# Mixture-of-experts encoder layer, one core: the item loops end one item earlier, and the last item's rows and both partial sums are added by TensorE

## The chip, the core and the metric

The kernel runs on one core of a Trainium2 chip. The metric is the device time of one execution in microseconds, lower is better. TensorE (PE) multiplies matrices into PSUM, VectorE (DVE), ScalarE (ACT) and GpSimd (POOL) do the elementwise work, and SyncE (SP) issues most of the DMAs.

## The reference

One post-norm layer over 1024 tokens of width 1024. A mixing part (pooling, convolution and memory attention) gives `x`, and then:

```python
scores = sigmoid(xt @ w_router)
_, idx = top_k(scores + router_bias, 8)          # 64 experts
gates = sel / sum(sel) * 2.5
for each block of 128 token rows of one expert e:
    h = silu(xb @ w_gate[e]) * (xb @ w_up[e])    # 1024 -> 256
    y = (h @ w_down[e]) * g
    acc = acc.at[tok].add(y)
out = layer_norm(alpha * x + acc + shared_expert(x)) # g2, b2
```

The number of blocks depends on the data. All values are float32.

## The kernel before

The mixing part and the router run first. The expert part is a list of items, each of 128 token rows times one expert. Items 0 to 7 are the shared expert's tiles, whose results go to DRAM with plain DMAs. Items from 8 (`NT`) on are routed ones, and `n_items`, read from the router's table, is their end. In the profiled execution it is 103: 1236 down matmuls at 12 an item, and 2304 gate/up matmuls at 24 for each of the steps 8 to 103.

Each engine has its own loop over the items, two to an iteration (`step_pe`, `step_act`, `step_v`), ordered by semaphores. Step `i` on TensorE transposes the gathered rows of item `i+1` (`rows_transposed`), transposes the hidden tile of item `i-1`, does `gate_up(i)` (24 matmuls), and `down(i-1)` (12 matmuls). `step_act(i)` writes the output of item `i-2` from PSUM to `ysb`, slot `i` modulo 2 (line 917), and `step_v` forms the low halves of the split operands. The loops run while `n_items` is at least `i`, so the last step has `i = n_items`: its `gate_up` is of an item that does not exist, and its `down` is of the last real one. After the loop, ScalarE (line 985) and VectorE (line 1470) write one half each of the last item's `ysb`.

GpSimd runs `fetch`: it gathers rows (`xg`, line 647), loads an item's list of tokens and gates into `idx` (line 640), and adds an item's `ysb` to DRAM by an indirect DMA with addition (line 657). There are two partial sums in DRAM, `sum_d[0]` and `sum_d[1]`: items of even number add to one and odd items to the other. There are 95 such scatters.

The closing part: SyncE waits (line 495) until all scatters but the last have landed and loads the half that the last item does not touch into `early`, in two DMAs of 2 MB (line 502). It then waits until the last scatter has landed and all engines are done (line 504), and loads the other half, tile by tile, into `late_` (line 506, eight DMAs of 512 KB). TensorE adds both into PSUM with the identity as stationary operand, in plain float32 (`add_part`, line 1860), for six of the eight tiles of 128 tokens. Tiles 4 and 6 (`ADDED`) are added by VectorE (line 1509). The LayerNorm of each tile: for tiles 0 and 7 VectorE takes the moments (`moments`, line 1498); for tiles 1 to 6 ScalarE does, in two passes (lines 1002 to 1012). GpSimd forms the power -1/2 (line 696), and VectorE normalises in two passes (`normalise`, lines 1486, 1490 and 1493). SyncE stores the tile (line 509). PSUM has four pairs of banks for the tiles; tile `t` of 4 and later waits for the first pass of tile `t-4`.

Of the kernel before, what the change touches and what calls it, by code (L numbers as in the profile page):

```python
# [14 lines left out]
F = mybir.dt.float32  # L15
# [4 lines left out]
ALU = mybir.AluOpType  # L20
# [29 lines left out]
ADDED = (4, 6)  # L50
# [6 lines left out]
def build(nc, a, out):  # L57
# [9 lines left out]
    with ctx:  # L67
# [79 lines left out]
        early = at("early", 96, [128, NT, D])  # L147
        late_ = at("late_", 0, [128, NT, D])
# [138 lines left out]
        s_endR = sem("s_endR")  # L287

        s_early = [sem(f"s_early{n}") for n in range(2)]
        s_late = [sem(f"s_late{t}") for t in range(NT)]  # L290
# [3 lines left out]
        s_added = sem("s_added")  # L294
# [67 lines left out]
        def _(sp):  # L362
# [138 lines left out]
            for n in range(2):  # L501
                sp.dma_start(early[:, 4 * n:4 * n + 4], rows_of(past % 2, 4 * n, 4)).then_inc(s_early[n], 16)
            sp.wait_ge(s_endC, 3)
            sp.wait_ge(s_endR, 1)
            for t in range(NT):
                sp.dma_start(late_[:, t:t + 1], rows_of((past + 1) % 2, t, 1)).then_inc(s_late[t], 16)
# [7 lines left out]
        def _(g):  # L514
# [174 lines left out]
            past = g.value_load(nit[0:1, 1:2], min_val=E, max_val=MAX_ITEMS - NT)  # L689
            for s in range(2):  # L690
                g.wait_ge(s_xg[s], 16 * ((past + 5 - s) // 2))
                g.wait_ge(s_yd[s], 16 * ((past + 1 - s) // 2))
            g.sem_inc(s_endR, 1)
# [6 lines left out]
        def _(act):  # L700
# [268 lines left out]
            with act.Fori(0, GROUPS) as group:  # L969
                with act.If(n_items > 2 * GROUP * group + NT + 3):  # L970
                    with act.Fori(0, GROUP) as pair:
                        jj = GROUP * group + pair
                        with act.If(n_items > 2 * jj + NT + 3):
                            step_act(2 * jj + NT + 4, 0, jj + 1)
                            with act.If(n_items > 2 * jj + NT + 4):
                                step_act(2 * jj + NT + 5, 1, jj + 1)


            late = act.value_load(nit[0:1, 2:3], min_val=E - 2, max_val=MAX_ITEMS - NT - 2)
            act.wait_ge(s_yd[0], 16 * ((late + 1) // 2))  # L980
            act.wait_ge(s_yd[1], 16 * (late // 2))
            slot = (n_items + 1) % 2
            act.wait_ge(s_dn, n_items)
            gate = idx[:, bass.ds((n_items + RING - 1) % RING, 1), 2:3].bitcast(F).rearrange("p a n -> p (a n)")
            nc.scalar.activation(ysb[:, bass.ds(slot, 1), 0:512].rearrange("p a n -> p (a n)"), ps[:, 5, :], ACT.Copy,
                                 scale=gate).then_inc(s_y, 1)
# [5 lines left out]
            for n, t in enumerate(range(1, NT - 1)):  # L992
                s = t % 2
                if t in ADDED:
                    act.wait_ge(s_added, ADDED.index(t) + 1)
                    y = acc[:, t]
                else:
                    act.wait_ge(s_pc, t + 1 - len([u for u in ADDED if u < t]))
                    y = ps[:, 2 * (t % 4):2 * (t % 4) + 2, :].rearrange("p a n -> p (a n)")
# [17 lines left out]
        def _(v):  # L1017
# [371 lines left out]
            def item_tables_out():  # L1389
                v.wait_ge(s_tabp, 1)  # L1390
                step(V.tensor_copy(tab[:].rearrange("p a b -> p (a b)"),
                                   ps[0:1, 7, 0:3 * TAB]))
                step(V.tensor_copy(nit[0:1, 0:1], endE[0:1, NE - 1:NE]))
                step(V.tensor_scalar(nit[0:1, 1:2], endE[0:1, NE - 1:NE], float(NT), None, ALU.subtract))
                step(V.tensor_scalar(nit[0:1, 2:3], endE[0:1, NE - 1:NE], float(NT + 2), None, ALU.subtract))
                settle()
                v.sem_inc(s_tabs, 1)
# [58 lines left out]
            with v.Fori(0, GROUPS) as group:  # L1456
                with v.If(n_items > 2 * GROUP * group + NT - 1):
                    with v.Fori(0, GROUP) as pair:
                        jj = GROUP * group + pair
                        with v.If(n_items > 2 * jj + NT - 1):  # L1460
                            step_v(2 * jj + NT, 0)
                            with v.If(n_items > 2 * jj + NT):
                                step_v(2 * jj + NT + 1, 1)
            settle()
            v.wait_ge(s_h, n_items + 1)
# [3 lines left out]
            gate = idx[:, bass.ds((n_items + RING - 1) % RING, 1), 2:3].bitcast(F).rearrange("p a n -> p (a n)")  # L1469
            V.tensor_scalar(ysb[:, bass.ds((n_items + 1) % 2, 1), 512:D].rearrange("p a n -> p (a n)"), ps[:, 6, :],  # L1470
                            gate, None, ALU.mult).then_inc(s_y, 1)
# [4 lines left out]
            def summed(t):  # L1476
                if t in ADDED:
                    return acc[:, t]
                return ps[:, 2 * (t % 4):2 * (t % 4) + 2, :].rearrange("p a n -> p (a n)")
# [26 lines left out]
            def add(t):  # L1506
                v.wait_ge(s_early[t // 4], 16)
                v.wait_ge(s_late[t], 16)
                step(V.tensor_tensor(acc[:, t], early[:, t], late_[:, t], ALU.add))
                settle()  # L1510
                v.sem_inc(s_added, 1)

            for t in range(NT):
                if t + 2 in ADDED:
                    add(t + 2)
# [5 lines left out]
            v.wait_ge(s_pc, NT - len(ADDED))  # L1521
# [5 lines left out]
        def _(pe):  # L1527
# [318 lines left out]
            with pe.Fori(0, GROUPS) as group:  # L1846
                with pe.If(n_items > 2 * GROUP * group + NT - 1):
                    with pe.Fori(0, GROUP) as pair:
                        jj = GROUP * group + pair
                        with pe.If(n_items > 2 * jj + NT - 1):  # L1850
                            step_pe(2 * jj + NT, 0, jj + 1)
                            with pe.If(n_items > 2 * jj + NT):
                                step_pe(2 * jj + NT + 1, 1, jj + 2)
            pe.wait_ge(s_dn, n_items)
# [3 lines left out]
            def add_part(t, rows):  # L1858
                for h in range(2):
                    last = mm(ps[:, 2 * (t % 4) + h, :], ident[:], rows[:, t, h * 512:(h + 1) * 512],  # L1860
                              start=(rows is early), stop=(rows is late_))
                return last

            summed = [t for t in range(NT) if t not in ADDED]
            for t in summed[:4]:
                pe.wait_ge(s_early[t // 4], 16)
                add_part(t, early)
            for n, t in enumerate(summed):
                if n >= 4:
                    pe.wait_ge(s_acc, t - 3)  # L1870
                    pe.wait_ge(s_early[t // 4], 16)
                    add_part(t, early)
                pe.wait_ge(s_late[t], 16)
                add_part(t, late_).then_inc(s_pc, 1)
# [52 lines left out]
```

## Time and profile before

| | us |
|---|---|
| median of 3 runs | 1392.77 |
| lowest, highest | 1388.06, 1400.06 |
| profiled execution, its time | 1394.81 |
| profiled execution, its span | 1393.2 |
| PE busy | 1316.1 (94%) |
| DVE busy | 956.1 (69%) |
| ACT busy | 795.5 (57%) |
| POOL busy | 498.6 (36%) |

The span runs from the first to the last instruction of the profiled execution, and its time is 1.61 us more. A row of a timeline gives where an instruction, or several of one kind, began, and for how long they ran. What stands in brackets is the idle time of that engine ahead of them and what ended it. A float32 matmul leaves more than one record in the trace, so counts of records and of calls in the code are told apart below. The mean granted clock of TensorE over the span is 0.972 of full speed.

### The profile page before, as it was taken

The page shows a single profiled execution, that of the slowest core. Times are in us where ns is not written, and L with a number is a line of the kernel's source. Part 1 is how long each engine was busy: PE and PEld are TensorE (multiplying, and loading weights), DVE is VectorE, ACT ScalarE, POOL GpSimd, SP SyncE. Part 2 cuts the span into 40 slices and gives each one's busy share as a digit, 9 for nine tenths or more (in the row PEclk, how much of TensorE's full clock was granted, in tenths as well). Part 3 has the DMA queues.
Part 4 walks back from the last instruction along what each step waited for, and adds up shares of the span by engine and source line. Part 5 has one row for each costly group of instructions (what it writes and reads, how often), then busy time and mean ns, then how long its engine had stood idle before and what let it go on. Part 6 is the DMA issues. An engine that isn't in the chain of part 4 may idle for free.

```text
span 1393.2 us, 25748 instructions
## 1 busy us (share of the span) xinstructions
PE 1316.1 (94%) x6395; PEld 1088.1 (78%) x6396; DVE 956.1 (69%) x1109; ACT 795.5 (57%) x1055; POOL 498.6 (36%) x444
## 2 busy tenths in 40 slices
PE   8989877999988999999999999999999999999974
PEld 6877765788876888888888888888888888888851
DVE  5798884767663777775777556647669579777727
ACT  4122274232235777766777556647678578777724
POOL 0000164265572333433343334333433343343322
PEclk9999988899998999999999999999999999999988
DMA  6121203232358899988999789778889899999665
GB/s 245 34 88 61 112 40 120 85 92 62 107 168 303 314 330 299 334 297 246 307 338 350 240 238 320 233 225 277 298 275 357 257 337 334 332 330 319 185 190 228
DMA packets 77970, 324.13 MB, mean 233 GB/s; under 512 B 22560, under 2 KB 24768, under 8 KB 52720
## 3 DMA queue, kind: packets, MB, share of 16 engines
q1 hardware_dynamic: 43056, 251.05, 48.5%
q0 software_dynamic: 33728, 68.47, 21.0%
q10 hardware_dynamic: 1152, 4.19, 0.7%
q8 instruction: 17, 0.28, 0.1%
q14 instruction: 17, 0.14, 0.0%
HBM read 290.51 MB, written 67.72 MB: 257 GB/s over the span
## 4 chain that ended last, share of the span: by engine, by line
PE 81%; DMA 5%; DVE 5%; issue 2%; ACT 2%; POOL 2%; another core or an unknown queue 1%; ACTq 0%; SPq 0%; POOLq 0%; DVEq 0%
PE ps L1788 35%; PE ps L1806 18%; PE ps L1654 7%; PE ps L1533 6%; PE ps L1558 5%; PE ps L1734 3%; DMA raw<-in_w_up 3%; DVE cv L1118 2%; PE ps L1723 2%; PE ps L1819 1%; DMA xg<-x_d,idx 1%; PE ps L1570 1%; DMA sum_d<-ysb,idx 1%; DMA xin<-in_x 1%
## 5 line engine op out<-in xcount | busy, mean ns | idle before, releaser
L1788 PE MATMUL ps<-wgu,xTe 128*128 x2304 | 549.9, 394 | 1.9 <-ACT wgu L843 0.8
L1788 PEld LDWEIGHTS ps<-wgu,xTe 128*128 128x128 f32 x2304 | 426.3, 188 | 90.2 <-issue 5.0
L657 POOL DMA_INDIRECT sum_d<-ysb,idx x95 | 176.4, 1857 | 510.5 <-ACT ysb L917 439.0
L1806 PE MATMUL ps<-wdn,hT 128*128 (+1 forms) x1236 | 302.0, 394 | 0.1
L1401 DVE TENSOR_TENSOR wgu<-raw,wgu (+1 forms) x128 | 287.7, 2289 | 8.2 <-issue 3.4
L1806 PEld LDWEIGHTS ps<-wdn,hT 128*128 128x128 f32 x1236 | 234.3, 190 | 49.2 <-issue 0.6
L843 ACT CAST wgu<-raw (+1 forms) x128 | 247.0, 1930 | 2.4 <-SPq L445 2.3
L1406 DVE TENSOR_TENSOR xTe<-ps,xTe 128x512 fp32r<-128x512 f32 x194 | 124.6, 684 | 131.0 <-ACT xTe L912 131.0
L917 ACT ACTIVATE ysb<-ps,idx 128x512 f32<-128x512 f32 x188 | 119.3, 686 | 122.5 <-PE ps L1806 122.5
L1401 DVE TENSOR_TENSOR wdn<-raw,wdn x64 | 146.7, 2293 | 59.6 <-ACT wdn L905 59.6
L647 POOL DMA_INDIRECT xg<-x_d,idx x99 | 110.4, 1115 | 50.0 <-issue 35.0
L905 ACT CAST wdn<-raw x64 | 125.0, 1953 | 0.0
L963 ACT ACTIVATE hs<-ps 128x256 f32<-128x256 f32 x96 | 36.9, 384 | 145.0 <-PE ps L1788 145.0
L1558 PE MATMUL ps<-xT,whl 128*128 128x512 f32 x480 | 110.1, 390 | 0.0
L912 ACT CAST xTe<-ps 128x512 fp32r<-128x512 f32 x194 | 104.4, 598 | 4.3 <-PE ps L1533 3.9
L1558 PEld LDWEIGHTS ps<-xT,whl 128*128 128x128 f32 x480 | 89.9, 188 | 19.2 <-issue 0.4
L1654 PE MATMUL ps<-wo,mst 128*128 128x512 f32 x384 | 97.6, 415 | 7.0 <-POOL mst L551 4.3
L1533 PE MATMUL ps<-ident,xg 128*128 128x128 f32 x776 | 100.9, 273 | 2.2 <-issue 2.0
L1533 PEld LDWEIGHTS ps<-ident,xg 128*128 128x128 f32 x776 | 90.5, 140 | 15.3 <-issue 2.9
L1435 DVE TENSOR_TENSOR hx<-hs,ps 128x256 f32<-128x256 f32 x96 | 40.1, 418 | 89.7 <-ACT hs L963 89.7
L600 POOL DMA_INDIRECT list_d<-tg,addr x64 | 74.0, 1157 | 60.9 <-DVEq L1253 44.2
L1654 PEld LDWEIGHTS ps<-wo,mst 128*128 128x128 f32 x384 | 76.0, 201 | 23.8 <-issue 7.6
(230 smaller groups left out, 1162.9 us busy)
## 6 DMA issues: line engine op xcount, KB each, us to landing
raw<-in_w_gate SPq DMA_DIRECT2D x64, 1024.0 KB
raw<-in_w_up SPq DMA_DIRECT2D x64, 1024.0 KB
raw<-in_w_down SPq DMA_DIRECT2D x64, 1024.0 KB
wraw<-in_w_in SPq DMA_DIRECT2D x10, 512.0 KB, 3.3
xin<-in_x SPq DMA_DIRECT2D x8, 512.0 KB, 7.8
wraw<-in_w_kv SPq DMA_DIRECT2D x8, 512.0 KB, 3.3
wor<-in_w_out SPq DMA_DIRECT2D x4, 1024.0 KB, 8.5
xres<-in_x SPq DMA_DIRECT2D x8, 512.0 KB
```

The costliest lines, as they stand in the source:

```text
L647: g.indirect_dma_start(out=xg[:, c % 2], out_offset=None, in_=x1_d, in_offset=bass.IndirectOffsetOnAxis(ap=idx[:, c % RING, 0:1], axis=0), ...
L657: g.indirect_dma_start(out=sums, out_offset=bass.IndirectOffsetOnAxis(ap=idx[:, c % RING, c % 2:c % 2 + 1], axis=0), in_=ysb[:, c % 2], in ...
L843: nc.scalar.copy(wgu[:, v, 0, :, n * XD:(n + 1) * XD].rearrange("p a c n -> p (a c) n"), raw[:, bass.ds(slot_of(e, n), 1)].rearrange("p a ...
L905: nc.scalar.copy(wdn[:, v, 0].rearrange("p a c n -> p (a c) n"), raw[:, bass.ds(slot_of(e, 2), 1)].rearrange("p a (c n) -> p (a c) n", c=2 ...
L917: nc.scalar.activation(ysb[:, slot, b * 512:(b + 1) * 512], ps[:, bank + b, :], ACT.Copy, scale=scale).then_inc(s_y, 1)
L1401: V.tensor_tensor(dst, raw_, hi.bitcast(F), ALU.subtract).then_inc(done, 1)
L1406: last = V.tensor_tensor(xTe[:, s, 1, 4 * b:4 * b + 4], ps[:, b, :].rearrange("p (c n) -> p c n", c=4), xTe[:, s, 0, 4 * b:4 * b + 4].bitc ...
L1533: last = nc.tensor.transpose(ps[:, bank + c // 4, (c % 4) * 128:(c % 4 + 1) * 128], src[:, c * 128:(c + 1) * 128], ident[:])
L1558: last = mm(ps[:, b + h, :], wt[:, st, d], xT[:, mo, d, h * 512:(h + 1) * 512], start=(d == 0 and st == 0 and mo == 0), stop=(d == ND - 1 ...
L1654: last = mm(ps[:, project_bank(t, h), :], mixed(t)[:, st, c], wo[:, mo, c, h * 512:(h + 1) * 512], start=(first and c == blocks[0] and st ...
L1788: last = mm(ps[:, 2 + s, :], xTe[:, s, st, d], wgu[:, w, mo, d].rearrange("p a n -> p (a n)"), start=(d == 0 and st == 0 and mo == 0), sto ...
L1806: last = mm(ps[:, down_bank(i) + h, :], hT[:, s, st, c], wdn[:, w, mo, c, h * 512:(h + 1) * 512].rearrange("p a n -> p (a n)"), start=(c = ...
```

## The change

The loops of TensorE, ScalarE and VectorE end with step `n_items - 1`, and GpSimd's ends one `fetch` earlier. Behind the loops stands what the last step did for real items: the output of item `n_items-2`, the hidden transpose, the split and `down` of item `n_items-1`. The phantom `gate_up` and the phantom row transposes are gone. For ScalarE and VectorE this puts the output of item `n_items-2` behind the end of the loop.

The last item is no longer scattered. GpSimd writes the numbers 0 to 1023 to `count`, and VectorE compares them with the last item's token numbers, which gives a one-hot matrix `place` (128 rows of the item by 1024 tokens). SyncE, once the scatter of item `n_items-2` has landed, loads both halves tile by tile (`sumA` and `sumB`, 16 DMAs of 512 KB), with no wait on the other engines. For each of the eight tiles TensorE adds the tile of `sumA`, the product of the one-hot slice with `ysb`, and the tile of `sumB`, two halves each, in float32. VectorE's two additions are gone.

The core of the diff:

```diff
             for t in range(NT):
-                sp.dma_start(late_[:, t:t + 1], rows_of((past + 1) % 2, t, 1)).then_inc(s_late[t], 16)
+                for buf, half in ((sumA, (past + 1) % 2), (sumB, past % 2)):
+                    sp.dma_start(buf[:, t:t + 1], rows_of(half, t, 1)).then_inc(s_sum[t], 16)
...
-                        inner.enter_context(g.If(n_items > RING * q + r - 3))
+                        inner.enter_context(g.If(n_items > RING * q + r - 2))
                         fetch(q, r)
 
+            g.wait_ge(s_glo, 2 * NE)
+            g.wait_ge(s_dlo, NE)
+            g.iota(count[:], pattern=[[1, S]], base=0, channel_multiplier=0,
+                   allow_small_or_imprecise_dtypes=True).then_inc(s_count, 1)
...
             late = act.value_load(nit[0:1, 2:3], min_val=E - 2, max_val=MAX_ITEMS - NT - 2)
+            past = act.value_load(nit[0:1, 1:2], min_val=E, max_val=MAX_ITEMS - NT)
+            third = act.value_load(nit[0:1, 3:4], min_val=E - 3, max_val=MAX_ITEMS - NT - 3)
...
+            act.wait_ge(s_dn, past + NT - 1)
+            first_half_out(n_items % 2, 2)
+            act.wait_ge(s_ht, n_items)
+            rows = ps[:, 4, :].rearrange("p (a c n) -> p a c n", a=2, c=2)[:, bass.ds((n_items + 1) % 2, 1)]
+            nc.scalar.copy(hT[:, 0, 0], rows.rearrange("p a c n -> p (a c) n")).then_inc(s_hhi, 1)
...
+            v.wait_ge(s_dn, past + NT - 1)
+            second_half_out(n_items % 2, 2)
+            v.wait_ge(s_hhi, n_items)
...
+            v.wait_ge(s_count, 1)
+            step(V.tensor_copy(lastf[:], idx[:, bass.ds((n_items + RING - 1) % RING, 1), 0:1].rearrange("p a n -> p (a n)")))
+            settle()
+            step(V.tensor_scalar(place[:], count[:], lastf[:], None, ALU.is_equal))
...
-                        with pe.If(n_items > 2 * jj + NT - 1):
+                        with pe.If(n_items > 2 * jj + NT):
                             step_pe(2 * jj + NT, 0, jj + 1)
...
+            for c in range(4):
+                last = nc.tensor.transpose(ps[:, 4, c * 128:(c + 1) * 128],
+                                           hx[:, c // 2, (c % 2) * 128:(c % 2 + 1) * 128], ident[:])
+            last.then_inc(s_ht, 1)
...
             pe.wait_ge(s_endC, 3)
+            for t in range(NT):
+                pe.wait_ge(s_sum[t], 32)
+                if t >= 4:
+                    pe.wait_ge(s_acc, t - 3)
                 for h in range(2):
+                    cols = slice(h * 512, (h + 1) * 512)
+                    bank = ps[:, 2 * (t % 4) + h, :]
+                    mm(bank, ident[:], sumA[:, t, cols], start=True, stop=False)
+                    mm(bank, place[:, t * 128:(t + 1) * 128], ysb[:, bass.ds(slot, 1), cols].rearrange("p a n -> p (a n)"),
+                       start=False, stop=False)
+                    last = mm(bank, ident[:], sumB[:, t, cols], start=False, stop=True)
+                last.then_inc(s_pc, 1)
```

## Rows read from the trace of the kernel before

**Rows 1.** The page: the chain that ended last, share of the span by line.
```profile
PE ps L1788 35%; PE ps L1806 18%; PE ps L1654 7%; PE ps L1533 6%; PE ps L1558 5%; PE ps L1734 3%; DMA raw<-in_w_up 3%; DVE cv L1118 2%; PE ps L1723 2%; PE ps L1819 1%; DMA xg<-x_d,idx 1%; PE ps L1570 1%; DMA sum_d<-ysb,idx 1%; DMA xin<-in_x 1%
```

**Rows 2.** Timeline, 1329 to 1343 us: start us, us, engine, line, operation, xcount, idle before.
```profile
1329.10 0.38 ACT L963 ACTIVATE hs<-ps 128x256 f32<-128x256 f32 x1 [2.04 <-PE ps L1788]
...
1332.05 1.27 ACT L917 ACTIVATE ysb<-ps,idx 128x512 f32<-128x512 f32 x2 [2.56 <-PE ps L1806]
...
1332.64 5.71 PE L1788 MATMUL ps<-wgu,xTe 128*128 x24
...
1334.26 1.61 POOL L657 DMA_INDIRECT sum_d<-ysb,idx  x1 [2.89 <-ACT ysb L917]
...
1338.19 2.88 PE L1806 MATMUL ps<-wdn,hT 128*128 x12
...
1338.39 0.38 ACT L963 ACTIVATE hs<-ps 128x256 f32<-128x256 f32 x1 [3.84 <-PE ps L1788]
...
1340.81 1.01 SPq L502 DMA_DIRECT2D early<-sum_d  x2
...
1342.56 0.69 ACT L985 ACTIVATE ysb<-ps,idx 128x512 f32 x1 [3.79 <-issue]
```

**Rows 3.** Chain that ended last, 1341 to 1360 us: start us, us, what.
```profile
1341.36 0.29 ACTq L979
...
1341.92 0.11 ACTq L980
...
1344.18 11.24 DMA sum_d<-ysb,idx
...
1356.01 3.21 DMA late__123<-sum_d
```

**Rows 4.** Line 506, its DMAs: duration ns, first and last start; then landing us.
```profile
L506 SPq DMA_DIRECT2D late__123<-sum_d x8: 332/345/680, 1356.0 to 1359.9; - x8
DMA to landing us min/median/max: 3.2/7.3/9.8
```

**Rows 5.** Timeline, 1348 to 1358 us, TensorE: columns as in Rows 2.
```profile
1348.90 9.51 PE L1860 MATMUL ps<-early,ident 128*128 128x512 f32 x16 [7.83 <-DMA early<-sum_d]
...
1354.38 0.19 PEld L1860 LDWEIGHTS ps<-early,ident 128*128 128x128 f32 x1 [0.24 <-issue]
...
1357.39 0.19 PEld L1860 LDWEIGHTS ps<-early,ident 128*128 128x128 f32 x1 [0.24 <-issue]
```

**Rows 6.** Tile early, its matmuls: x count, ns min/median/max, first and last start us.
```profile
L1860 PE MATMUL ps<-early,ident x24: 592/593/1190, 1348.9 to 1377.1; 128*128 128x512 f32 x24
```

**Rows 7.** Two windows of 1 us: busy us by engine, granted clock, DMA share, GB/s.
```profile
1343.00:1344.00 1.00, 0.00 (x0) 0.00 (x0) 0.00 (x0) 0.45 (x2) 0.00 (x0) 0.75 0.98 373
1353.00:1354.00 1.00, 1.00 (x3) 0.38 (x2) 0.00 (x0) 0.00 (x0) 0.00 (x0) 0.63 1.11 315
```

**Rows 8.** Timeline, 1361 to 1386 us: columns as in Rows 2.
```profile
1361.37 1.30 DVE L1498 BATCH_NORM_STATS2 stat<-ps 128x6 f32<-128x512 f32 x2 [19.08 <-PE ps L1860]
...
1363.23 1.03 ACT L1002 ACTIVATE sq<-ps 128x1024 f32<-128x1024 f32 x1 [19.66 <-PE ps L1860]
...
1366.23 1.36 POOL L696 TENSOR_TENSOR rs<-mv,neghalf 128x1 f32<-128x1 f32 x1 [2.48 <-ACT mv L1012]
...
1369.03 0.54 POOL L696 TENSOR_TENSOR rs<-mv,neghalf 128x1 f32<-128x1 f32 x1 [1.43 <-ACT mv L1012]
...
1383.21 1.28 DVE L1490 SCALAR_TENSOR_TENSOR acc<-acc,lnst,g 128x1024 f32<-128x1024 f32 x1 [0.44 <-POOL rs L696]
...
1385.84 1.29 DVE L1498 BATCH_NORM_STATS2 stat<-ps 128x6 f32<-128x512 f32 x2
```

**Rows 9.** Groups by line and form: xcount, busy us, mean ns, idle before.
```profile
L551 POOL TENSOR_TENSOR mst<-mixA,mst 128x512 fp32r<-128x512 f32 x8 | 10.3, 1287 | 6.7 <-ACT mst L791 6.6
...
L575 POOL IOTA listE<- 128x64 f32 x1 | 0.2, 209 | 0.0
...
L1057 DVE TENSOR_SCALAR memin<-memin,mv 128x1024 f32<-128x1024 f32 x2 | 1.5, 811 | 0.8 <-POOL mv L535 0.8
```

More of the change, by code:

```diff
@@ L145, in build @@
         nit = at("nit", 201.875, [1, 8], I32)
-        early = at("early", 96, [128, NT, D])
-        late_ = at("late_", 0, [128, NT, D])
+        sumA = at("sumA", 96, [128, NT, D])
+        sumB = at("sumB", 0, [128, NT, D])
+        count = at("count", 136, [128, S])
+        place = at("place", 140, [128, S])
+        lastf = at("lastf", 192.125, [128, 1])
         acc = at("acc", 32, [128, NT, D])
@@ L1468, in _ @@
             v.wait_ge(s_dn, n_items)
-            gate = idx[:, bass.ds((n_items + RING - 1) % RING, 1), 2:3].bitcast(F).rearrange("p a n -> p (a n)")
-            V.tensor_scalar(ysb[:, bass.ds((n_items + 1) % 2, 1), 512:D].rearrange("p a n -> p (a n)"), ps[:, 6, :],
-                            gate, None, ALU.mult).then_inc(s_y, 1)
+            second_half_out((n_items + 1) % 2, 1)
+            settle()
             v.sem_inc(s_endC, 1)
@@ L1846, in _ @@
             with pe.Fori(0, GROUPS) as group:
[L1847 removed]
+                with pe.If(n_items > 2 * GROUP * group + NT):
                     with pe.Fori(0, GROUP) as pair:
                         jj = GROUP * group + pair
[L1850 removed]
+                        with pe.If(n_items > 2 * jj + NT):
                             step_pe(2 * jj + NT, 0, jj + 1)
[L1852 removed]
+                            with pe.If(n_items > 2 * jj + NT + 1):
                                 step_pe(2 * jj + NT + 1, 1, jj + 2)
+            slot = (n_items + 1) % 2
+            past = pe.value_load(nit[0:1, 1:2], min_val=E, max_val=MAX_ITEMS - NT)
+            pe.wait_ge(s_h, n_items)
+            pe.wait_ge(s_hlo, past + NT - 1)
+            for c in range(4):
+                last = nc.tensor.transpose(ps[:, 4, c * 128:(c + 1) * 128],
+                                           hx[:, c // 2, (c % 2) * 128:(c % 2 + 1) * 128], ident[:])
+            last.then_inc(s_ht, 1)
+            e = pe.value_load(tab[0:1, 0, bass.ds(past + NT - 1, 1)], min_val=0, max_val=E)
+            w = bass.ds(e % 2, 1)
+            pe.wait_ge(s_hhi, n_items)
+            pe.wait_ge(s_dhi, NE)
+            pe.wait_ge(s_y, 2 * n_items)
+            for st, mo in ((0, 0), (1, 0), (0, 1)):
+                if st == 1:
+                    pe.wait_ge(s_hlo, n_items)
+                if mo == 1:
+                    pe.wait_ge(s_dlo, NE)
+                for h in range(2):
+                    for c in range(2):
+                        last = mm(ps[:, 5 + h, :], hT[:, 0, st, c],
+                                  wdn[:, w, mo, c, h * 512:(h + 1) * 512].rearrange("p a n -> p (a n)"),
+                                  start=(c == 0 and st == 0 and mo == 0), stop=(c == 1 and mo == 1))
+            last.then_inc(s_dn, 1)
             pe.wait_ge(s_dn, n_items)
```

91 lines of the change are left out of this document (36 added, 55 removed).

## The prediction

> **What bounds the kernel now.** I read the chain that ended last first. It is TensorE nearly all the way: the gate/up line alone is 35% of the span and the down line 18% [rows 1]. So in the loops only TensorE's work counts, and the change leaves every step but the last one as it is. What it does change is the closing stretch, so the second view is the timeline from 1329 us on. The reader is to see there that TensorE's last loop step holds a gate/up of 5.71 us, at 1332.64, for an item that doesn't exist, ahead of the last real down at 1338.19 [rows 2]. Behind it comes a relay: ScalarE writes its half of the last item's output at 1342.56 [rows 2], the last scatter runs from 1344.18 for 11.24 us, and only then the first DMA of `late_` starts, at 1356.01, and takes 3.21 us [rows 3]. The third stretch is the eight tiles: VectorE's first statistics start at 1361.37 and the last tile's at 1385.84 [rows 8], so 24.47 us for seven tiles, 3.5 us each, and 7.36 us more to the end of the span at 1393.2.
>
> So the change aims at the relay, and pays in the tiles. I cost both against the profiled execution's span, 1393.2 us. That execution's own time is 1394.81, 2.04 above the median of the runs, 1392.77. The median is what I predict, so I add the difference of the spans to it.
>
> **When the loads can start now.** They wait for the scatter of item 101 (`n_items-2`), no more for that of 102.
> Before, its output was written inside the loop from 1332.05 for 1.27 us, that is until 1333.32; its scatter began at 1334.26, 0.94 later; and SyncE issued the `early` loads at 1340.81, 6.55 after that [rows 2]. In the changed kernel this output is written behind ScalarE's loop. ScalarE's way out of the loop can be read: its last instruction in the loop starts at 1338.39 and the first behind it at 1342.56, so 4.17 us [rows 2], with TensorE done in the meantime (1338.19 + 2.88 = 1341.07), so that it is mostly tests and register loads. The changed kernel makes two more register loads there, at 0.56 us (from 1341.36 to 1341.92 [rows 3]), 1.12 in all. The loop's last instruction is then the one at 1329.10 [rows 2]. 1329.10 + 4.17 + 1.12 = 1334.39; its half takes 0.69 [rows 2], to 1335.08. VectorE's half has a shorter way and is not last. The scatter begins at 1335.08 + 0.94 = 1336.02, and the first load is issued at 1336.02 + 6.55 = 1342.57. Against the 1356.01 of `late_` that is 13.44 us earlier; against `early`, 1.76 later.
>
> **When TensorE can begin.** Tile 0 needs two DMAs of 512 KB. One took 3.21 [rows 3]. The eight of line 506 landed between 3.2 us after the first issue at 1356.0 and 9.8 after the last at 1359.9, so 10.5 us for seven more, 1.5 each [rows 4]. 3.2 + 1.5 = 4.7: tile 0 is there at 1347.3. The other conditions lie ahead of that. Down(102): ScalarE's copy of the hidden tile follows its output at 1335.08 and takes under half a microsecond; down takes 2.88 [rows 2]; it ends near 1339. The four transposes and the restated waits on TensorE lie under ScalarE's way out. `place`: GpSimd is free at 1336.02 + 1.61 = 1337.6 [rows 2]; I give it ScalarE's 4.17 to leave its loop, 1341.8. The trace has no iota of 1024 columns. Below it is the one of 64 columns, 0.21 us, above it that times 16, 3.3 us; the two-input GpSimd operation on 512 columns, 1.29, is 2.6 for 1024 [rows 9]. I take the top, 1345.1. The comparison goes by VectorE's 0.81 for 128x1024 [rows 9], then its half of the output, about ScalarE's 0.69 [rows 2]: 1346.6. That is 0.7 us ahead of the data, so I cost `count`, `place`, the copy to `lastf` and the third register value at nothing; their cover is the DMA of tile 0, and past it each microsecond costs one.
>
> **What the sums cost.** This is the step that decides. The 12 calls on `early` left 24 records [rows 6]: a float32 matmul of 512 columns is two records. At full clock their weight loads start at 1354.38 and at 1357.39 with 7 intervals between them [rows 5]: 0.43 us a record. The changed kernel makes 6 calls a tile, 12 records, 5.16 us; eight tiles 41.3 us. Before it was 6 tiles of 4 calls, 48 records or 20.6 us, and the 16 that ran first lay under the last scatter. I take the one-hot product at the same price as the identity's: same type, same shape. 5.16 is more than the 3.5 us at which tiles left before, so TensorE sets the pace. The loads don't: 16 of them at 1.5 are 24 us; they would bind only above 2.6 each.
> The clock: it fell to half within the microsecond at 1343, 2 us after down had ended, and rose in the one at 1353 [rows 7], 4.9 us after TensorE had begun again. The 16 records took 9.51 [rows 5] where 16 x 0.43 plus 0.16 of drain is 7.04, so the half clock cost 2.5 us. Now TensorE is idle from about 1339 to 1347.3, 8 us against 7.83 [rows 5], so I take 2.5 again; with no fall it would be 0.
>
> **The end.** Tile 6 is summed at 1347.3 + 2.5 + 7 x 5.16 = 1385.9, tile 7 at 1391.1. Tile 6's LayerNorm is then last. ScalarE follows by 0.1, and from its start to GpSimd's are 3.00 us (1363.23 to 1366.23 [rows 8]). GpSimd's power took 0.54 at 1369.03 and 1.36 at 1366.23 [rows 8]; with VectorE idle by then I take 0.54, and 0.03 on. VectorE's two passes up to the next statistics: 1383.21 to 1385.84, 2.63 [rows 8]. 1385.9 + 6.3 = 1392.2, past tile 7's 1391.1. Then 7.36 as before: **1399.6**, 6.4 us over 1393.2.
> The Trainium skill's page "SBUF — State Buffer", section "SBUF: two separate sides", says that VectorE and GpSimd share a pair of SBUF ports as an exclusive lock, taken by a VectorE operation with two SBUF inputs; by it the short power is right here, and without it the end would be 0.8 later.
> VectorE's two additions that go away are worth nothing while TensorE is the slower. The phantom gate/up (5.71) and its transposes bring nothing by themselves either: the loads hang on the scatter of 101.
> As a check by differences: tile 0 is summed at 1347.3 + 2.5 + 5.2 = 1355.0, 6.3 before its first statistics at 1361.37; seven tiles cost 36.1 for 24.5, 11.6 more; tile 6's LayerNorm adds 1.1. -6.3 + 11.6 + 1.1 = +6.4. The median: 1392.77 + 6.4 = **1399.2**.
>
> **The rivals.**
> *The LayerNorm stays the bound* (faster side). If a record cost what the split operands' do, 5.71 / 24 = 0.24 us [rows 2], a tile would be 2.9 us, under 3.5. Then tile 0 is summed at 1347.3 + 2.9 + 2.5 = 1352.7, and the 31.8 us from 1361.37 to the end follow: 1384.5, a median of 1384. It turns at 3.5 / 12 = 0.29 us a record. Against it stand 24 records at 0.43 on the same kind of operand [rows 5, 6]; for it only that `place` against `ysb` is new, and it is a third of the records. Chance 0.09.
> The Trainium skill's page "FP8 and Floating Point Precision", section "TensorE Precision Notes", gives four passes to true float32; that rule speaks against this rival.
> *GpSimd is late with `count`*. If its way out of the loop is twice ScalarE's, 8.3 us, then 1337.6 + 8.3 + 3.3 + 1.5 = 1350.7 and everything moves by 3.4: a median of 1402.6. It decides from 0.7 us beyond my sum on. The trace doesn't show GpSimd's exit, as the last scatter hid it. Chance 0.12.
> The Trainium skill's "GPSIMD Engine Reference", section 2.1, adds about 6 us to the first call of a freshly loaded GpSimd routine; iota ran early in the kernel at 0.21 us with no such gap, and if it were due again here the end would be 5.3 us later.
> *The clock stays at half* through the tiles: 96 x 0.43 less the 2.5 counted, 38.8 more, a median of 1438. The rows show it rising under the same records back to back [rows 7]. Chance 0.03.
> *The change doesn't bring the loads forward*: if the scatter of 101 lands as slowly as that of 102, 11.24 [rows 3], the loads start 5 us later and the median is 1404. That one ran against 4 MB of loads and this one doesn't. Chance 0.06.
>
> **How the numbers follow.** Forecast as reasoned, 0.63; the rivals 0.30; other things 0.07. Within the forecast, the clock's 2.5 can be absent, tile 0 can land 1.5 earlier, ScalarE's exit 1 us shorter or longer, GpSimd's power 1.1 longer; and the 3 runs before differ by 12 us, so a median of them is sure to some 4 us. That makes 1392 to 1405 for it alone. The range reaches toward both sides' rivals: 1389 to 1407. About 1%, 13.9 us, is what a measurement tells from no change: under 1378.8 is faster, over 1406.7 slower. Neither the forecast nor the first rival passes that. Faster 0.03, within 1% 0.88, slower 0.09.
>
> **What would show it.** Line 506's loads issued about 13 us earlier than before, relative to the loop's end; 96 float32 records at 0.43 us in the tile stretch where there were 48; TensorE busy nearly without a gap from tile 0 to 7; tiles stored every 5.2 us; ScalarE and VectorE waiting for TensorE. What would make it wrong: records of the one-hot product at another spacing, TensorE's first sum waiting for VectorE and not for a DMA, or a first load later than 9 us after the last output in the scatter.

## The result and the profile after

| | before | changed |
|---|---|---|
| median, us (20 runs each) | 1394.03 | 1399.6 |
| lowest to highest, us | 1388.06 to 1401.32 | 1394.5 to 1406.58 |
| ratio | 1 | 1.0045, 95% interval 1.003 to 1.006 |
| span of the profiled execution, us | 1393.2 | 1398.1 |
| PE busy, us | 1316.1 | 1327.3 |
| float32 records of the sums | 48 | 96 |

The changed kernel is slower by 0.45%, 6.3 us by the ratio and 5.6 by the two medians. In a second comparison, on another occasion, the ratio was 1.0044 (1.002 to 1.0068).

The executions differ by a few microseconds in the long loops, which the change leaves alone (the common point of the next sentence lies between 1322.67 and 1329.86 us in the profiles below). So all places below are also given from one common point, the start of ScalarE's last instruction for the gate of item 102 (the one at 1329.10 in [rows 2]), written as +x. From there to the end of the span it is 64.1 us before and 71.2 after (70.4 in the second profile of the changed kernel): 6 to 7 us, as much as the whole difference. Up to VectorE's statistics of tile 7 it is 56.7 before and 62.9 after (62.1 in the second profile), 6.1 and 5.4 us. The rest, about 0.9, lies behind those statistics, and there the profile of the kernel before is the odd one: 7.4 us to the end, against 8.2 to 8.4 in each of the twelve other profiles, also in those that have its closing part.

The stretch that answers to [rows 2, 3], timeline of the changed kernel (start us, us, engine, line, operation, idle before):

```profile
1326.93 0.38 ACT L966 ACTIVATE hs<-ps 128x256 f32<-128x256 f32 x1 [2.09 <-PE ps L1808]
...
1332.38 0.69 ACT L988 ACTIVATE ysb<-ps,idx 128x512 f32 x1 [5.06 <-issue]
...
1333.62 5.48 PE L1894 MATMUL ps<-wdn,hT 128*128 x12 [3.56 <-ACT hT L997]
1334.00 1.62 POOL L654 DMA_INDIRECT sum_d<-ysb,idx  x1 [4.86 <-ACT ysb L988]
1336.76 0.99 POOL L688 IOTA count<- 128x1024 f32 x1 [1.13 <-issue]
...
1338.16 0.76 DVE L1497 TENSOR_SCALAR place<-count,lastf 128x1024 f32<-128x1024 f32 x1
...
1339.44 0.75 DVE L1483 TENSOR_SCALAR ysb<-ps,idx 128x512 f32 x1 [0.53 <-PE ps L1894]
1340.30 0.34 SPq L503 DMA_DIRECT2D sumA<-sum_d  x1
...
1345.00 2.04 PE L1909 MATMUL ps<-sumA,ident 128*128 128x512 f32 x2 [5.90 <-DMA sumB<-sum_d]
...
1352.51 1.02 PE L1909 MATMUL ps<-sumA,ident 128*128 128x512 f32 x2
```

From the common point, 1326.93: item 101's output by ScalarE at +5.45, its scatter at +7.07, the first load at +13.37, TensorE's first sum at +18.07. GpSimd writes `count` at 1336.76, VectorE compares at 1338.16 and writes its half of the last output at 1339.44, all well ahead of 1345.00. At 1352.51 tile 1 begins, so tile 0 took 7.5 us.

The waits in the same stretch (engine and line, for whom, us in total, times, longest):

```profile
ACT sq L1013 <- PE ps L1912: 28.5, 6, 17.3
...
PE ps L1909 <- DMA sumB<-sum_d: 5.9, 1, 5.9
```

TensorE waits for the loads once, for 5.9 us. After that it is waited for: ScalarE's statistics stand 28.5 us for it, 17.3 of them before their first tile and 2.24 ahead of each of the five others. Before, with tiles at 3.5 us [rows 8], it was the other way round: TensorE stood twice until VectorE had freed a pair of banks, as this row of the same view of the kernel before shows:

```profile
PE ps L1860 <- DVEq L1492: 4.9, 2, 2.9
```

The chain that ended last in the changed kernel, in order of time (start us, us, what):

```profile
1352.67 0.86 PE ps L1909 x2
...
1357.82 0.86 PE ps L1909 x2
...
1382.72 0.87 PE ps L1912 x2
...
1383.61 1.12 ACT sq L1013 x2
...
1386.60 0.55 POOL rs L699
...
1389.89 1.22 DVE stat L1527 x2
```

Tile 1 begins at 1352.67, tile 2 at 1357.82: 5.15 us. The chain is float32 matmuls without a gap up to the end of tile 6's, at 1383.59, and from there tile 6's LayerNorm, then tile 7's.

Granted clock in five windows of 1 us (behind the busy times of the five engines stand the granted clock as a share of full speed, the DMA share and GB/s):

```profile
1332.00:1333.00 1.00, 0.00 (x0) 0.00 (x0) 0.18 (x1) 0.62 (x2) 0.00 (x0) 0.78 0.23 63
1334.00:1335.00 1.00, 1.00 (x3) 0.77 (x3) 0.00 (x0) 0.00 (x0) 1.00 (x1) 0.50 0.00 0
1339.00:1340.00 1.00, 0.10 (x1) 0.00 (x0) 0.56 (x1) 0.57 (x1) 0.00 (x0) 0.81 0.16 29
1342.00:1343.00 1.00, 0.00 (x0) 0.00 (x0) 0.00 (x0) 0.00 (x0) 0.00 (x0) 0.90 0.98 373
1349.00:1350.00 1.00, 1.00 (x3) 0.37 (x2) 0.00 (x0) 0.00 (x0) 0.00 (x0) 0.69 1.03 418
```

A value between 0.50 and 1.00 is a window in which the level changed. The clock fell in the window at 1332 (0.78), while TensorE waited for the hidden tile. It stood at 0.50 under the last down (the window at 1334) and rose in the one at 1339 (0.81). It fell again in the one at 1342 (0.90), while TensorE waited for the loads, and rose in the one at 1349 (0.69), 4 us after the sums had begun. So the last down ran at the lower level, 1.2 GHz, and so did most of tile 0.

### The profile page after: what moved, and what is told of

It is laid out like the page before. It is cut to its first block, busy times and chain, and to the rows that moved or that the text cites. A ratio compares the mean times of both kernels' runs of the same rounds, so it can differ in the third digit from the quotient of the medians.

```text
span 1398.1 us, 25622 instructions
## 1 busy us (share of the span) xinstructions
PE 1327.3 (95%) x6413; PEld 1091.2 (78%) x6414; DVE 950.9 (68%) x1108; ACT 793.7 (57%) x1051; POOL 498.8 (36%) x442
## 4 chain that ended last, share of the span: by engine, by line
PE 87%; DVE 4%; DMA 2%; ACT 2%; issue 2%; POOL 2%; another core or an unknown queue 1%; ACTq 0%; SPq 0%; DVEq 0%; POOLq 0%
PE ps L1808 37%; PE ps L1826 19%; PE ps L1674 7%; PE ps L1553 7%; PE ps L1578 5%; PE ps L1754 3%; DVE cv L1129 2%; PE ps L1743 2%; PE ps L1839 1%; PE ps L1909 1%; PE ps L1910 1%; PE ps L1912 1%; PE ps L1590 1%; DMA xin<-in_x 1%
## 5 line engine op out<-in xcount | busy, mean ns | idle before, releaser
L1808 PE MATMUL ps<-wgu,xTe 128*128 x2280 | 543.2, 394 | 3.7 <-issue 2.4
L1808 PEld LDWEIGHTS ps<-wgu,xTe 128*128 128x128 f32 x2280 | 421.5, 188 | 90.4 <-issue 6.3
L644 POOL DMA_INDIRECT xg<-x_d,idx x98 | 110.9, 1131 | 51.0 <-issue 26.9
L597 POOL DMA_INDIRECT list_d<-tg,addr x64 | 74.7, 1167 | 58.8 <-DVEq L1264 42.1
```

Source lines behind the costliest of these rows:

```text
L644: g.indirect_dma_start(out=xg[:, c % 2], out_offset=None, in_=x1_d, in_offset=bass.IndirectOffsetOnAxis(ap=idx[:, c % RING, 0:1], axis=0), ...
L1808: last = mm(ps[:, 2 + s, :], xTe[:, s, st, d], wgu[:, w, mo, d].rearrange("p a n -> p (a n)"), start=(d == 0 and st == 0 and mo == 0), sto ...
```

## The experiments

All are ratios to the kernel before, run beside each of them on the same occasion, with their 95% intervals. The last column is the stretch from the common point to the end of the span in the one profiled execution of each; the 64.1 of the kernel before holds the short end of 7.4 us, and with the others' 8.3 it would be 65.0.

| kernel | ratio | from the common point to the end, us |
|---|---|---|
| before | 1 | 64.1 |
| changed, twice | 1.0045 (1.003 to 1.006), 1.0044 (1.002 to 1.0068) | 71.2, 70.4 |
| no_onehot | 0.9959 (0.9932 to 0.9986) | 58.8 |
| hoist | 0.9985 (0.9961 to 1.0009) | 64.4 |
| hoist_adds | 0.9979 (0.9962 to 0.9997) | 60.7 |
| split | 0.9956 (0.9938 to 0.9974) | 57.1 |
| warm | 1.0049 (1.003 to 1.0067) | 69.2 |
| half_first | 1.012 (1.0088 to 1.0151) | 81.7 |
| loop_end | 1.0022 (1.0003 to 1.004) | 68.4 |
| loop_end_registers | 1.0015 (0.9998 to 1.0032) | 67.1 |
| early_registers | 1.0009 (0.9992 to 1.0027) | 71.1 |
| no_last_scatter | 0.9999 (0.9977 to 1.002) | 64.7 |

### The changed kernel again

> The changed kernel as it is, beside the others on the same chip. A ratio to the kernel before near 1.0045, and its tile stretch as in its first trace: the first sum waits for the DMA of tile 0, then the float32 records stand 0.43 us apart without a gap.

1.0044, as expected: the first load at +13.4, the first sum at +18.2, the tiles 5.15 us apart. Tile 0 took 6.6 us here and not 7.5, as the clock rose sooner after the sums had begun.

### Without the one-hot product

```diff
                     mm(bank, ident[:], sumA[:, t, cols], start=True, stop=False)
-                    mm(bank, place[:, t * 128:(t + 1) * 128], ysb[...], start=False, stop=False)
                     last = mm(bank, ident[:], sumB[:, t, cols], start=False, stop=True)
```

> The one-hot product is left out of the sums, so the last item's rows are missing from the output; everything else, place and its cover too, stays. Theory (TensorE's float32 records set the pace of the tiles): 8 records a tile instead of 12, 3.44 us for 5.16, tile 6 summed about 12 us earlier, close to the pace of the LayerNorm (3.5 us a tile before), so 11 to 12 us off the changed kernel, a ratio of 0.996 to the kernel before. Rival (the 16 loads or the LayerNorm set the pace): within 2 us of the changed kernel, 1.003 to 1.0045.

Measured 0.9959: 12 us off the changed kernel. Its timeline (TensorE's first sum, then VectorE's first pass of two neighbouring tiles):

```profile
1341.13 2.04 PE L1909 MATMUL ps<-sumA,ident 128*128 128x512 f32 x2 [7.37 <-DMA sumB<-sum_d]
...
1356.83 1.28 DVE L1519 SCALAR_TENSOR_TENSOR acc<-ps,lnst,g 128x1024 f32<-128x1024 f32 x1 [0.70 <-POOL rs L699]
...
1360.27 1.28 DVE L1519 SCALAR_TENSOR_TENSOR acc<-ps,lnst,g 128x1024 f32<-128x1024 f32 x1 [0.72 <-POOL rs L699]
```

The tiles are 1360.27 - 1356.83 = 3.44 us apart, which is 8 records of 0.43, and not 5.15. So the count of records sets the pace. 3.44 is close to the 3.5 of the kernel before, but it is still TensorE's and not the LayerNorm's: TensorE runs without a gap from tile 0 to tile 7, and ScalarE's statistics wait 0.52 us for it at each tile from 2 on.

### The one-hot products of four tiles first

```diff
+            for t in range(4):
+                place_rows(t)            # place x ysb, start=True, both halves
             for t in range(NT):
-                pe.wait_ge(s_sum[t], 32)
                 if t >= 4:
                     pe.wait_ge(s_acc, t - 3)
+                    place_rows(t)
+                pe.wait_ge(s_sum[t], 32)
...
```

> The one-hot products of tiles 0 to 3 are issued first, as they need no load: 16 of the 96 records then lie in TensorE's wait for tile 0 (5.9 us in the trace), and the clock has risen by the time the data is there. Nothing is left out. Theory: from tile 0's landing, 4 x 3.44 + 3 x 5.16 = 29.2 us to tile 6's sum instead of 38.5, so 9.3 us off the changed kernel, a ratio of 0.998. If only the clock's fall mattered: 2.5 us off, 1.003. If loads or the LayerNorm set the pace: no change, 1.0045.

Measured 0.9985 (0.9961 to 1.0009, which holds the expected 0.998), and 6 to 7 us less than the changed kernel in the last stretch, not 9.3. The timeline says where the missing 2.5 us stayed:

```profile
1338.05 7.13 PE L1904 MATMUL ps<-ysb,place 128*128 x16 [1.34 <-ACTq L1003]
1338.38 0.34 SPq L503 DMA_DIRECT2D sumA<-sum_d  x1
...
1345.02 1.02 PE L1917 MATMUL ps<-sumA,ident 128*128 128x512 f32 x2
```

The 16 records took 7.13 us from 1338.05 and ended at 1345.18, while the loads had been issued at 1338.38 and by the 4.7 us of the changed kernel were there at about 1343.1. The products of tiles 1 to 3 held tile 0 up. Nothing is lost in TensorE's sum of work by that, as it stands still nowhere from 1338.05 on; but its work can't start before 1338.05, when the last output is written, and my expectation began to count at the data. Between the last output (+13.5) and the data (+18.1 in the changed kernel) there are 4.6 us, and the 16 products need 6.9.

### VectorE adds both sums of five tiles

```diff
+            def add(t):                  # t in (3, 4, 5, 6, 7), behind normalise(t - 3)
+                v.wait_ge(s_sum[t], 32)
+                step(V.tensor_tensor(sumA[:, t], sumA[:, t], sumB[:, t], ALU.add))
...
```

> As the kernel that issues the one-hot products of tiles 0 to 3 first, and VectorE adds both sums of tiles 3 to 7 (1.22 us each) so that TensorE has one product with the identity there instead of two. Nothing is left out. Theory (TensorE's 96 float32 records are the work that sets the end): 76 records, 8.6 us less of TensorE, but VectorE's 2.7 us a tile and 6.2 us of additions come near it, so 4 to 5 us off that kernel, a ratio of 0.995. Rival (VectorE's additions cost as much as they save, as it must normalise too): 0.998 to 1.0.

Its last stretch is 3.7 us shorter than hoist's (60.7 for 64.4), near the 4 to 5 expected, though 0.6 of it is only that TensorE's first product starts sooner (+12.9 for +13.5). The ratio says otherwise: 0.9979 is the rival's number, its interval (0.9962 to 0.9997) leaves out the theory's 0.995, and it doesn't tell this kernel from hoist's 0.9985. VectorE is now close to full, with 4.2 to 4.7 us busy in each 5 from 1355 on, and TensorE waits for it four times. How much the additions bring in the median stays open.

### All of one half first

```diff
-            for t in range(NT):
-                for buf, half in ((sumA, (past + 1) % 2), (sumB, past % 2)):
+            for buf, half in ((sumA, (past + 1) % 2), (sumB, past % 2)):
+                for t in range(NT):
                     sp.dma_start(buf[:, t:t + 1], rows_of(half, t, 1)).then_inc(s_sum[t], 16)
```

> The changed kernel, with the 16 loads in another order: all eight tiles of sumA, then all of sumB. The same bytes, from the same moment. Theory (only tile 0's landing counts of the loads, and they pass through one queue in order): tile 0's second half is the ninth DMA instead of the second, 8 to 9 us later, and the whole end with it: a ratio of 1.010 to 1.011. Rival (the loads are hidden behind TensorE's pace): no change, 1.0045.

```profile
1324.80 0.38 ACT L966 ACTIVATE hs<-ps 128x256 f32<-128x256 f32 x1 [2.09 <-PE ps L1808]
...
1338.41 4.32 SPq L503 DMA_DIRECT2D sumA<-sum_d  x8
1342.98 4.13 SPq L503 DMA_DIRECT2D sumB<-sum_d  x8
...
1353.20 2.04 PE L1909 MATMUL ps<-sumA,ident 128*128 128x512 f32 x2 [17.33 <-DMA sumB<-sum_d]
```

The first load at +13.6, close to the changed kernel's +13.4, but the first sum at +28.4 instead of +18.1, and 1.012 (from four executions only). Of the loads tile 0's landing is what counts, and their order alone is worth 10 us of the end. From the first issue to tile 0's second half it is 14.8 us, nine half-megabytes.

### TensorE kept busy while it waits

```diff
             pe.sem_inc(s_endC, 1)
 
+            pe.wait_ge(s_g2, 32)
+            for n in range(5):
+                mm(ps[:, 7, :], ident[:], g2[:, 0:512], start=True, stop=True)
             pe.wait_ge(s_endC, 3)
```

> The changed kernel, with five float32 matmuls of 512 columns on g2 into a free bank behind the last down, while TensorE waits for tile 0; their results are not used. Theory: the granted clock stays at its upper level, tile 0 takes 5.2 us instead of 7.7, 2.5 us off, a ratio of 1.0027. Rival: the clock falls or the added matmuls delay tile 0, 1.0045 or more.

```profile
1347.77 1.10 PE L1912 MATMUL ps<-sumA,ident 128*128 128x512 f32 x2 [1.43 <-DMA sumB<-sum_d]
...
1353.00 1.02 PE L1912 MATMUL ps<-sumA,ident 128*128 128x512 f32 x2
```

```profile
1347.00:1348.00 1.00, 0.23 (x1) 0.26 (x2) 0.00 (x0) 0.00 (x0) 0.00 (x0) 1.00 0.94 234
1348.00:1349.00 1.00, 1.00 (x3) 0.42 (x3) 0.00 (x0) 0.00 (x0) 0.00 (x0) 1.00 1.05 389
```

The clock was at 1.00 when tile 0's sums ran (windows 1347 and 1348), and they took 5.2 us (1347.77 to 1353.00) for the changed kernel's 7.5 and 6.6. The last stretch is 69.2 for 71.2 and 70.4. The ratio, 1.0049, is the rival's: its interval reaches down to 1.003 only and leaves out the theory's 1.0027. TensorE stood still for 1.4 us between the added matmuls and tile 0's landing, so they did not hold it up. So the clock's price at this place is shown in the trace, and that it can be had in the median is not.

### Only the loops shortened

The loops of the changed kernel with the closing part of the kernel before; the last item is scattered.

```diff
-                        inner.enter_context(g.If(n_items > RING * q + r - 2))
-                        fetch(q, r)
+                        inner.enter_context(g.If(n_items > RING * q + r - 3))
+                        with g.If(n_items > RING * q + r - 2):
+                            fetch(q, r, False)      # gather and list of the next ones
+                        add_rows(q, r - 3)
```

> Only the first part of the change: the loops end with the last real item, but that item is scattered, and the closing part (early, late_, two tiles added by VectorE) is that of the kernel before. Theory (ScalarE's way out of the loop, not the phantom gate/up, is what the last output waited for): the last scatter starts 14.2 us after ScalarE's last loop instruction of item 102 instead of 15.1, so about 1 us faster than before, 0.999. Rival (the phantom gate/up and its transposes, 6.6 us of TensorE, were on the path): 6 us faster, 0.995 to 0.996.

Neither: 1.0022, slower. Timeline of this kernel (the common point, last scatter, loads, TensorE's sums):

```profile
1329.86 0.39 ACT L968 ACTIVATE hs<-ps 128x256 f32<-128x256 f32 x1 [2.09 <-PE ps L1821]
...
1343.27 1.58 POOL L660 DMA_INDIRECT sum_d<-ysb,idx  x1 [4.71 <-DVE ysb L1489]
1343.34 1.01 SPq L505 DMA_DIRECT2D early<-sum_d  x2
1354.27 4.04 SPq L509 DMA_DIRECT2D late__123<-sum_d  x8
...
1354.44 8.63 PE L1917 MATMUL ps<-early,ident 128*128 128x512 f32 x16 [13.25 <-DMA early<-sum_d]
...
1362.91 2.31 PE L1917 MATMUL ps<-late__123,ident 128*128 128x512 f32 x5
```

The last scatter does start sooner (+13.41 for +15.08 before), and `late_` is issued sooner (+24.4 for +26.9). But `early` is issued later (+13.5 for +11.7 [rows 2]), it now goes out with the last scatter beside it, and TensorE can begin on its first half 11.1 us after its issue instead of 8.1. TensorE's 16 records on it begin at +24.6 (before +19.8), take 8.5 us, and `late_` is added right behind them, at +33.05 (before +30.17). The late half's landing isn't what it waited for; its own sums of the early half are. Dropping the phantom gate/up brought none of the rival's 6 us. That the scatter beside the loads is what slowed them is not shown by an edit of its own, but the two traces in which none starts there agree (8.1 before, 8.0 without the last scatter, below).

### The same with the register loads ahead of the loops

```diff
+            late = act.value_load(nit[0:1, 2:3], ...)   # and past, third; on VectorE past, third
             item_hi(NT, 0)
...
-            late = act.value_load(nit[0:1, 2:3], ...)   # behind the loop
```

> The kernel with only the shortened loops and the old closing part, and the register loads ahead of the loops. Theory (its loss is that item 101's output moved behind ScalarE's loop, which delays early's issue by 1.8 us, and what follows in the one queue): early is issued 1.5 us sooner after ScalarE's last loop instruction, and 1.5 us come off, 1.001. Rival: 1.0022 as without.

1.0015, last stretch 67.1 for 68.4. In the trace `early` is issued at +11.9, 1.6 us sooner, and TensorE begins on the late half at +31.75 for +33.05: 1.3 us, near the theory's 1.5. `late_` goes out at +16.7 here, 10 us sooner than in the kernel before, and TensorE begins on it 1.6 us later than there. The direction is the theory's; the two ratios are not told apart.

### The changed kernel with those register loads ahead

> The changed kernel, with the register loads that it has behind ScalarE's and VectorE's loops put ahead of them. Theory: ScalarE's way from its last loop instruction to item 101's output is shorter by the loads (5.45 us to about 3.9), the first DMA of the sums is issued 11.9 us after that instruction instead of 13.4, tile 0 and the end move by the same 1.5 us: a ratio of 1.0034. Rival (the way out of the loop doesn't matter): 1.0045 and the first DMA at 13.4.

```profile
1328.31 0.38 ACT L969 ACTIVATE hs<-ps 128x256 f32<-128x256 f32 x1 [2.09 <-PE ps L1808]
...
1332.11 0.69 ACT L988 ACTIVATE ysb<-ps,idx 128x512 f32 x1 [3.41 <-issue]
...
1340.30 0.34 SPq L503 DMA_DIRECT2D sumA<-sum_d  x1
...
1345.79 2.04 PE L1909 MATMUL ps<-sumA,ident 128*128 128x512 f32 x2 [7.80 <-DMA sumB<-sum_d]
...
1353.81 1.02 PE L1909 MATMUL ps<-sumA,ident 128*128 128x512 f32 x2
```

ScalarE's output of item 101 is at +3.80 (5.45 before the edit) and the first load at +11.99, as expected. But tile 0 took 5.5 us to land instead of 4.7, and its first sum is at +17.48, 0.6 us earlier and not 1.5. Tile 0 then took 8.0 us (tile 1 begins at 1353.81) for the changed kernel's 7.5 and 6.6, as the clock rose only in the window at 1351, so tile 1 begins at +25.50 for +25.58 and +24.79. That is where the rest of the gain went in this profile, and its last stretch is no shorter, 71.1. The ratio of 1.0009 (0.9992 to 1.0027) is lower than the 1.0034 that the theory gives, and nothing in the one trace accounts for that; the changed kernel was not run on the same occasion. It is left open.

### The kernel before, without its last scatter

```diff
-                        inner.enter_context(g.If(n_items > RING * q + r - 3))
+                        inner.enter_context(g.If(n_items > RING * q + r - 2))
...
-                g.wait_ge(s_xg[s], 16 * ((past + 5 - s) // 2))
-                g.wait_ge(s_yd[s], 16 * ((past + 1 - s) // 2))
+                g.wait_ge(s_xg[s], 16 * ((past + 4 - s) // 2))
+            g.wait_ge(s_yd[0], 16 * (past // 2))
+            g.wait_ge(s_yd[1], 16 * ((late + 1) // 2))
```

> The kernel before, with its loops and its closing part, but the last item is not scattered and nobody waits for it: its rows are missing from the output. Theory (early's 4 MB, issued first, hold the one queue; the last scatter's 11 us lie mostly beside them): the first tile of late_ is the ninth half-megabyte from early's issue, 14.7 us after it as in the run with all of sumA first, instead of 18.4, so 3.7 us faster, a ratio of 0.9973. Rival (the relay through the last scatter is on the path with its whole length): late_ is issued 12.5 us earlier and the end follows, 0.991.

0.9999 (0.9977 to 1.002): neither. Timeline (the common point, both loads, TensorE's sums, first statistics):

```profile
1322.72 0.38 ACT L965 ACTIVATE hs<-ps 128x256 f32<-128x256 f32 x1 [2.03 <-PE ps L1790]
...
1334.51 1.01 SPq L502 DMA_DIRECT2D early<-sum_d  x2
...
1337.15 7.07 SPq L506 DMA_DIRECT2D late__123<-sum_d  x8
...
1342.52 10.11 PE L1862 MATMUL ps<-early,ident 128*128 128x512 f32 x16 [7.83 <-DMA early<-sum_d]
...
1352.47 7.03 PE L1862 MATMUL ps<-late__123,ident 128*128 128x512 f32 x16
...
1354.46 1.29 DVE L1500 BATCH_NORM_STATS2 stat<-ps 128x6 f32<-128x512 f32 x2 [18.55 <-PE ps L1862]
```

`late_` is issued at +14.4 instead of +26.9, 12.5 us earlier, and it brings nothing. TensorE begins on `early` at +19.8, as before, needs 10.1 us for its 16 records with the clock down at first, and adds `late_` without a gap at +29.75; before it did so at +30.17. The statistics start at +31.74 for +32.27, and tile 7's at +56.4 for +56.7. So the relay through the last scatter, 11.24 us in the chain [rows 3], was covered but for half a microsecond by the loads and sums of the other half.

### A version that beats both

One-hot products first; the last item's rows as a rounded part and a remainder; VectorE adds tiles 4 and 6; register loads ahead of the loops.

```diff
+            nc.scalar.activation(yr[:, 0, 0:512], ps[:, 5, :], ACT.Copy, scale=gate).then_inc(s_y, 1)
...
+            V.tensor_scalar(yr[:, 0, 512:D], ps[:, 6, :], gate, None, ALU.mult).then_inc(s_y, 1)
+            v.wait_ge(s_y, 2 * n_items + 2)
+            step(V.scalar_tensor_tensor(yr[:, 1], ps[:, 5:7, :].rearrange("p a n -> p (a n)"), gate, yr[:, 0].bitcast(F),
+                                        ALU.mult, ALU.subtract))
...
+                    for part in range(2):
+                        mm(ps[:, 2 * (t % 4) + h, :], place[:, t * 128:(t + 1) * 128],
+                           yr[:, part, h * 512:(h + 1) * 512], start=(part == 0), stop=False)
...
```

> A version meant to beat both: one-hot products of tiles 0 to 3 first, the last item's rows kept as a rounded part and a remainder and multiplied in the split format (two records of 0.23 us for two of 0.43), VectorE adds tiles 4 and 6, and the register loads of ScalarE and VectorE stand ahead of their loops. Theory: first load 1 us earlier (12.3 us after ScalarE's last loop instruction for 13.4), tiles at 4.4 us or less, then bound by the LayerNorm's chain: 7 us faster than the kernel before, a ratio of 0.995 to 0.994. Rival (the split's extra pass on VectorE, 1.3 us, and the additions eat it): 0.998.

```profile
1325.01 0.39 ACT L972 ACTIVATE hs<-ps 128x256 f32<-128x256 f32 x1 [2.08 <-PE ps L1824]
...
1337.00 0.34 SPq L506 DMA_DIRECT2D sumA<-sum_d  x1
...
1337.44 5.51 PE L1921 MATMUL ps<-yr,place 128*128 128x512 f32 x16 [2.79 <-DVEq L1511]
...
1342.79 1.02 PE L1940 MATMUL ps<-sumA,ident 128*128 128x512 f32 x2
```

0.9956 (0.9938 to 0.9974): 6 us faster than the kernel before, 12 faster than the changed one. The expected 0.995 lies in the interval. Which of its four parts brings how much was not taken apart. The 16 records of four tiles took 5.51 us, partly at the lower clock, for 7.13 in float32. The first load is at +12.0 and tile 0's first sum, behind the one-hot products, at +17.8.

## Why the prediction was right

The forecast was 1399.2 us, 6.4 above the kernel before; the ratio gives 6.3, the medians 5.6. That the median itself, 1399.6, lies within 0.4 us of the forecast is in part luck: the base of 1392.77 was the median of 3 runs, and on the 1394.03 of the 20 the same sum gives 1400.4. Its steps, each from the common point (1329.10 in the prediction), beside the first profile of the changed kernel:

| step | predicted | measured |
|---|---|---|
| scatter of item 101 starts | +6.9 | +7.1 |
| first load issued | +13.5 | +13.4 |
| TensorE's first sum | +18.2 | +18.1 |
| tile to tile | 5.16 us | 5.15 us |
| tile 6 summed, from the first sum | 38.6 us | 38.6 us |
| tile 7's statistics, from there | 6.3 us | 6.2 us |
| the sum of these, against 56.7 before | +6.4 us | +6.1 us |
| from those to the end | 7.36 us | 8.3 us |

**The price of the sums** carried the forecast, and the run without the one-hot product shows it: 4 records a tile fewer, 12 us less. The first rival, that the LayerNorm stays the bound, needed records of 0.29 us or less; they took 0.43, the one-hot's too. The two smaller rivals are out as well: the clock rose in the window at 1349, and the scatter of item 101 landed after 6.0 us and not 11.24.

**The clock** cost 2.3 us, near the 2.5 that was taken (7.5 us for tile 0 where 5.2 was had in the kernel that kept TensorE busy). It is no fixed price: in the second profile it was 1.4. That it would fall once more, ahead of the last down, was missed: the down took 5.48 us instead of the 2.88 that I put down. It lay beside the scatter of item 101 and cost nothing.

**The cover of `place`** was much larger than I had it. GpSimd was out of its loop 1.1 us after its scatter, where I gave it ScalarE's 4.17, and the iota took 0.99 where I took the top bound, 3.3. VectorE was done at 1340.2, 4.8 us ahead of the data, not 0.7. The rival of a late GpSimd is out. The 6 us that the Trainium skill's "GPSIMD Engine Reference", section 2.1, gives for the first call of a freshly loaded routine didn't show: the iota, used once early in the kernel, began 1.1 us after the scatter and took 0.99.

**What I said of the gain was right in the sum and wrong in its reason.** The sentence "the change aims at the relay" and the 13.44 us that the loads come earlier suggest that the last scatter was what the end waited for. In the kernel without it nothing was gained (0.9999), and with only the loops shortened the kernel was slower. What brought tile 0 forward, from the landing of its last part at +30.2 to +18.1, takes both: without the last scatter both halves can be loaded at once, and because they come tile by tile tile 0 is there after two of the sixteen loads. With the same loads in another order 10 us of it are gone. This step of the reasoning failed, though no term of the sum hung on it. I took the relay from the chain of waits, which named one of two paths of nearly the same length; the other, 4 MB of `early` and TensorE's 16 records on it, lay 0.9 us under it (1348.90 + 9.51 = 1358.4 against 1359.3 [rows 3, 5]) and was in my own rows. The forecast escaped this because it compared where the stretch ends, not what was taken out.

Not tried is the interleaved order with the last scatter kept. With only the loops shortened and the registers loaded ahead, that scatter had landed by +16.7, 3 us behind the changed kernel's first load, and with it no one-hot product is needed. From the run without the one-hot product, 58.8 us with its first load at +13.6, the estimate is a stretch of 62 us, under the 65 of the kernel before.

**The end** was 0.9 us longer than 7.36, and not by the change. From tile 7's statistics to the end of the span it is 8.2 to 8.4 us in all twelve other profiles, among them the three with the closing part of before (8.3 without the last scatter, 8.4 and 8.3 with only the loops shortened). The 7.36 came from the one profile of the kernel before. GpSimd's power of tile 6 took the short time that was assumed (0.55 at 1386.60), and the store landed 2.6 us after its issue, as before. Why that one profile is shorter behind the store isn't in the rows, and stays open.

## What to carry to other kernels

Before a step is taken off the chain of waits, look for the path that lies just under it: here an 11 us scatter could go without any gain, because the loads and sums of the other half ended only 0.9 us earlier. Work moved onto TensorE in plain float32 costs two records of 0.43 us for each 512 columns (at full clock), so additions by the identity have to be counted like any matmul: 96 records were 41 us in a stretch where the other engines needed 3.5 us a tile. When several things must be complete for the first tile, load them interleaved by tile, and let TensorE do what needs no load while it waits.

## What was not expected of the hardware

- The granted clock fell and rose twice within 17 us (windows 1332 to 1349 above). The last down took 5.48 us at the lower level, and 4.4 to 5.5 in the other kernels with the same way to it; with the register loads ahead of the loops, where TensorE's wait was 1.9 us for 3.6, it took 4.6, 4.6 and 3.0.
- A scatter with addition of 128 rows took 6 us from its start to its landing with little beside it (1334.00 to 1339.99 in the chain of the changed kernel), and 11.24 with 4 MB of loads that had begun 3.4 us sooner [rows 3]. In turn, TensorE could begin on the first 2 MB of `early` 11.1 us after their issue with a scatter starting at the same moment, and 8.1 us after it with one that started 3.4 us later, which is what it took with no last scatter at all (8.0). Each is one trace.
- GpSimd's iota of 1024 float32 columns took 0.99 us, against 0.21 for 64. An estimate from these two sizes: 0.8 ns a column and 0.16 us fixed; two of 2 columns, at 236 us in the trace before, took 0.17 and 0.16.
